# RWKV loop of a two-block model: rates, decays and products per chunk of 64 tokens instead of per block of 128

## The reference, cut to what matters

```python
def rwkv_prepare(rw, p):
    r, k, v, wl, al, gl = jnp.split(rw, RWKV_SPLITS, axis=-1)
    kk = heads(k * p['k_k'])                     # then normed per head
    w_lat = jnp.tanh(wl)
    for each direction:
        w = -jax.nn.softplus(-(w0 + w_lat @ w2)) - 0.5
        decay = jnp.exp(-jnp.exp(w))             # = exp(-exp(-0.5) * sigmoid(w0 + w_lat @ w2))
        a = jax.nn.sigmoid(a0 + al @ a2)
        k_dir = k * (1.0 + (a - 1.0) * p['k_a'])

def rwkv_scan(...):                              # for each direction
    def step(S, inp):
        sa = jnp.einsum('bhvk,bhk->bhv', S, kk_t)
        S = S * w_t - sa * (kk_t * a_t) + v_t * k_t
        return S, jnp.einsum('bhvk,bhk->bhv', S, r_t)
```

## Time and profile before

| | us |
|---|---|
| median of 3 runs (2999.21 to 3003.76) | 2999.66 |
| profiled execution | 3002.31 |
| its span | 3000.5 |
| TensorE busy in the span | 2717.9 (91%) |
| VectorE busy | 1418.4 (47%) |
| ScalarE busy | 516.1 (17%) |
| GpSimd busy | 162.8 (5%) |

### The profile page before, as it was taken

How to read it: one execution, slowest core, us unless ns; L and a number is a source line. 1 busy time by engine, 2 the same in 40 slices (tenths; PEclk the granted TensorE clock), 3 DMA queues, 4 the chain that set the end, 5 groups by cost and what they waited for, 6 DMA issues and landing times.

```text
span 3000.5 us, 46544 instructions
## 1 busy us (share of the span) xinstructions
PE 2717.9 (91%) x20206; PEld 1974.1 (66%) x20206; DVE 1418.4 (47%) x2486; ACT 516.1 (17%) x1033; POOL 162.8 (5%) x112
## 2 busy tenths in 40 slices
PE   7989999998999898999999988997778769999996
PEld 3643788886645445888884743546777733788885
DVE  3153655525004436555424365254444463877624
ACT  2121100001013322000001032013333211122100
POOL 0000000000000000000000000003333200000000
PEclk9979999999998989999999977997999979999998
DMA  5313222233120002232234101200000013222231
GB/s 189 97 36 98 71 85 85 67 100 100 57 84 1 1 30 83 93 96 84 58 99 128 42 15 56 56 1 2 4 4 4 4 57 98 71 85 84 67 91 53
DMA packets 219563, 190.34 MB, mean 63 GB/s; under 512 B 8667, under 2 KB 216956, under 8 KB 219360
## 3 DMA queue, kind: packets, MB, share of 16 engines
q1 hardware_dynamic: 219066, 187.27, 20.2%
q10 hardware_dynamic: 294, 0.09, 0.0%
HBM read 185.25 MB, written 2.10 MB: 62 GB/s over the span
## 4 chain that ended last, share of the span: by engine, by line
PE 81%; DVE 12%; issue 2%; ACT 2%; DVEq 0%; DMA 0%; POOLq 0%; POOL 0%; ACTq 0%; SPq 0%
PE psum L1138 26%; PE psum L335 18%; PE psum L1348 13%; PE psum L365 4%; PE psum L2041 4%; PE psum L2048 3%; PE psum L778 2%; PE psum L800 2%; DVE sbuf L277 1%; PE psum L786 1%; PE psum L776 1%; DVE sbuf L290 1%; PE psum L2118 1%; PE psum L1751 1%; DVE sbuf L2431 1%
## 5 line engine op out<-in xcount | busy, mean ns | idle before, releaser
L1138 PE MATMUL psum<-sbuf 128*128 128x256 f32 x3696 | 810.6, 383 | 9.9 <-DVE sbuf L1197 6.5
L1138 PEld LDWEIGHTS psum<-sbuf 128*128 128x128 f32 x3696 | 708.7, 192 | 110.8 <-DVE sbuf L1197 7.7
L335 PE MATMUL psum<-sbuf 128*128 128x512 f32 (+5 forms) x1424 | 542.4, 543 | 22.7 <-DVEq L434 22.5
L335 PEld LDWEIGHTS psum<-sbuf 128*128 128x128 f32 (+3 forms) x1424 | 264.5, 187 | 295.8 <-issue 257.1
L1348 PE MATMUL psum<-sbuf 128*128 128x256 f32 x1848 | 405.2, 382 | 12.4 <-DVE sbuf L1365 6.8
L1348 PEld LDWEIGHTS psum<-sbuf 128*128 128x128 f32 x1848 | 353.8, 192 | 63.5 <-DVE sbuf L1365 7.6
L1222 DVE TENSOR_TENSOR sbuf<-sbuf,psum 128x256 f32<-128x256 f32 x462 | 177.7, 415 | 205.7 <-PE psum L1138 204.5
L2048 PE MATMUL psum<-sbuf 64*64 64x64 f32 x4992 | 204.8, 232 | 32.6 <-issue 19.1
L2041 PE MATMUL psum<-sbuf 64*64 64x64 f32 (+1 forms) x4544 | 180.0, 233 | 50.3 <-DVE sbuf L2409 30.6
L2048 PEld LDWEIGHTS psum<-sbuf 64*64 64x64 f32 x4992 | 180.0, 143 | 44.2 <-issue 38.1
L2041 PEld LDWEIGHTS psum<-sbuf 64*64 64x64 f32 x4544 | 164.5, 141 | 57.1 <-DVE sbuf L2409 32.0
(11 more groups left out here) (232 smaller groups left out, 2516.7 us busy)
## 6 DMA issues: line engine op xcount, KB each, us to landing
sbuf<-in_w_mod_dram SPq DMA_DIRECT2D x24, 1024.0 KB, 5.2
sbuf<-in_w_ffn_gate_dram SPq DMA_DIRECT2D x22, 1024.0 KB, 5.5
sbuf<-in_w_ffn_up_dram SPq DMA_DIRECT2D x22, 1024.0 KB, 7.3
sbuf<-in_w_ffn_down_dram SPq DMA_DIRECT2D x32, 704.0 KB, 6.2
sbuf<-in_w_up_dram SPq DMA_DIRECT2D x22, 1024.0 KB, 5.4
sbuf<-in_w_out_dram SPq DMA_DIRECT2D x12, 1024.0 KB, 5.2
sbuf<-in_w_in_dram SPq DMA_DIRECT2D x12, 1024.0 KB, 5.3
sbuf<-in_w_down_dram SPq DMA_DIRECT2D x16, 704.0 KB, 6.3
```

What stands on the lines that cost most here:

```text
L335: mm = pe.matmul(bank, w[:, q, c0:c0 + m], rhs(k0 + q), start=start and q == 0, stop=stop and q == kc - 1)
L1138: mm = pe.matmul(bank, w[:, q, :], rhs[:, q, :], start=q == 0, stop=q == 3)
```

## The change

Preparation goes by chunk, both directions together, and three chunks ahead. Iterations n = -3, -2, -1 take the place of the separate prologue. In iteration n TensorE runs `latents(n + 3)` at the end of level 3 and `cums(n + 3)` at level 4, ScalarE `rate(n + 3)` and `exps(n + 3)` there, so every chunk has both. `latents` has two products of 512 columns, direction 0 into partitions 0 to 63 and direction 1 into 64 to 127 of bank 4, and eight of 64 columns. `cums` stays at four products of 256 columns, now for one chunk of both directions. `exps` has six exponentials of 256 elements in a main chunk instead of three of 512 for each block and direction. AR, B, K and GAM have buffers for four chunks. VectorE makes `products(n + 2)` as a generator and issues its instructions behind the updates of the levels: 5, 2, 1, 1, 1 of them. GpSimd's `kka` has two instructions of 256 elements and stands first in its iteration. `gram_l(g)` waits for the products of chunk g, made an iteration earlier. `kv`, `turn_v` wait for `exps` of chunk n + 2.

```diff
-        def latents(b, d):
-            tok = block_tokens(b, d)
-            pe.matmul(k.bank[4], WA[0:33, tok], W2A[0:33, d, :], start=True, stop=True)
-            for f in range(4):
-                mm = pe.matmul(k.bank[5][:, f * P:(f + 1) * P], W2A[64:97, d, f * P:(f + 1) * P], WA[64:97, tok],
-                               start=True, stop=True)
+        def latents(c):
+            if c >= 1:
+                wait("exps", c)
...
+            for d in range(2):
+                pe.matmul(k.bank[4][HEADS[d], :], WA[0:33, chunk_tokens(c, d)], W2A[0:33, d, :], start=True, stop=True)
+            for d in range(2):
+                for f in range(4):
+                    mm = pe.matmul(k.bank[5][:, column(4 * d + f)], W2A[64:97, d, f * P:(f + 1) * P], WA[64:97, chunk_tokens(c, d)],
+                                   start=True, stop=True)
             mm.then_inc(sems["latent_done"], 1)
...
         def gram_l(g):
-            wait("prods", prep(g // 2, 1))
+            wait("prods", g + 1)
...
-                if lv == 4:
-                    prepare(n, 1)
+                if lv == 4 and c < NCH:
+                    cums(c)
...
-                if lv == 3:
-                    if n == -1:
-                        wait("exps", 2)
-                    prepare(n, 0)
+                if lv == 3 and c < NCH:
+                    latents(c)
...
+        def exps(c):
+            wait("cums_done", c + 1)
+            cum = k.psum[:, 2048:3072].rearrange("p (f w d t) -> p f w d t", f=4, w=2, d=2)
+            for d in range(2):
+                incl, excl, tile = cum[:, :, 0, d], cum[:, :, 1, d], AR[c % 4][:, d]
+                act.activation(tile[:, :, 0, :], incl if d else excl, ACT.Exp, scale=-DECAY if d else DECAY)
+                act.activation(B[c % 4][:, d], excl if d else incl, ACT.Exp, scale=DECAY if d else -DECAY)
+                if main(c):
+                    act.activation(tile[:, :, 1, :], excl if d else incl, ACT.Exp, scale=-DECAY if d else DECAY)
+            act.activation(GAM[c % 4].unsqueeze(3), cum[:, :, 0, :, CH - 1:CH], ACT.Exp, scale=DECAY).then_inc(sems["exps"], 1)
...
+        def products(c):
+            Kf, Bf, rate, tile = K[c % 4], B[c % 4], RATE[c % 2], AR[c % 4]
+            flat4 = lambda ap: ap.rearrange("p d f t -> p (d f t)")
+            wait("exps", c + 1)
+            by_pair = lambda ap: ap.rearrange("p d f t -> p (d f) t")
+            dve.scalar_tensor_tensor(out=by_pair(Kf), in0=by_pair(rate), scalar=-1.0, in1=KA.unsqueeze(2).broadcast_to([P, 8, CH]),
+                                     op0=ALU.add, op1=ALU.mult).then_inc(sems["k_gain"], 1)
+            yield
+            for w, name in ((0, "KK"), (1, "R")):
+                for d in range(2) if w == 0 or main(c) else ():
+                    dve.tensor_tensor(tile[:, d, :, w, :], tile[:, d, :, w, :], src[name][:, :, chunk_tokens(c, d)], ALU.mult)
+                    yield
+            wait("k_gain", c + 1)
+            for d in range(2):
+                ins = dve.scalar_tensor_tensor(out=Kf[:, d], in0=Kf[:, d], scalar=1.0, in1=src["K"][:, :, chunk_tokens(c, d)],
+                                               op0=ALU.add, op1=ALU.mult)
+                if d == 0:
+                    yield
+            k.dve.link(ins)
+            yield
+            k.dve.link(dve.tensor_tensor(flat4(Kf), flat4(Kf), flat4(Bf), ALU.mult))
+            yield
+            wait("kka", c + 1)
+            dve.tensor_tensor(flat4(Bf), flat4(rate), flat4(Bf), ALU.mult).then_inc(sems["prods"], 1)
+            yield
...
                 if lv == 2 and 0 <= m < NCH - 1:
                     state(m)
-            if exps_in(n) is not None:
-                products(exps_in(n), 0)
+                for _ in range((5, 2, 1, 1, 1)[lv]):
+                    next(filler, None)
+            for _ in filler:
+                pass
```

## The result

The changed kernel takes 3008.52 us in the median (3003.02 to 3014.28, 10 runs), the kernel before 3000.64 (2997.03 to 3003.76, 10 runs): ratio 1.0026, 95% interval 1.0015 to 1.0036. It is slower; 2986 was predicted. The profiled execution after has a span of 3012.5 us, before 3000.5. It took 3014.28 us, the slowest of its ten and 5.8 us above the median, the one before 1.7 above, so about 4 of the 12.0 us are these two executions' own. The difference of 12.0 us lies in the prologue (+6.4) and the loop (+6.5), and the rest of the program is 0.9 us shorter.

The account below looks back on a forecast made before the run. TensorE was taken as the bound, stopped by VectorE's block of products. Terms -29.9 + 2 + 7.5 + 2 + 4.5 = -13.9 us took the median 2999.7 to 2986; own range 2979 to 2995 (chance 0.50), whole range 2972 to 3008.

Parts of the forecast that it names:

- Part 1: Loop, level-0 to level-1 and level-4 to level-0 updates: TensorE's stall behind VectorE's block of products goes, -29.9 us.
- Part 2: VectorE's products at their new places: level 0 costs +2 us (bounds 0 and +4), levels 1 to 3 cost 0.
- rival 1: Level 3, slower: B*rate is let in only after GpSimd's five loff instructions, +21 us, 3007; chance 0.18.
- rival 3: No change: K*B shows at level 2 (+5.6), the table switch at level 4 (+5), 2996.6 us; chance 0.15.
- Part 3: TensorE's latents and cums in the loop: 30.5 us before, 38.0 after, +7.5 (bounds -2.4 and +13.8).
- rival 2: TensorE's latents, faster: the two wide products share time, having different columns, 2974 us; chance 0.17.
- The upper bound: Case of Part 3: small latents follow behind the wide ones at 0.06 to 0.11 us each, +13.8 us.
- Part 4: ScalarE at level 4: exponentials come some 0.25 us late per main chunk, +2 us; the table load hides, 0.
- Part 5: Prologue, mostly at 1.2 GHz: latents and cums of its chunks cost more, +4.5 us (bounds +2 and +8).

Follow-up runs that it names:

- a_sched: Changed kernel with VectorE's products spread 5, 1, 1, 0, 2 over the levels instead of 5, 2, 1, 1, 1: 3004.66 us, ratio 1.0024 to the kernel before.
- a_quad: Changed kernel with each of its eight small latent products cut into two of 64 output channels: 2982.71 us, ratio 0.9950 to the kernel before.
- a_onetable: Changed kernel with the decays made by Sigmoid instead of Exp, no table switch in the loop (wrong numbers): 3011.16 us, ratio 1.0037 to the kernel before.
- a_lat_old: Changed kernel with old-shape latents per chunk, one 128-token product and four of 128 columns (direction 1 wrong): 2974.55 us, ratio 0.9917 to the kernel before.
- hybrid: Changed kernel with small latents as four products of 128 columns, one direction and two chunks at a time: 2993.07 us, ratio 0.9986 to the kernel before.

## Why the prediction was wrong, step by step

- **Part 1, the block goes (-29.9):** right. 29.1 us by the same four sums, no wait for the last product in the loop, the longest of the ten stretches U0 to U1 6.38 us.
- **Part 2, places on VectorE (+2):** wrong at level 1. "The second ends about when the next update is due: 0" holds only where TensorE is slow to bring that update. The half of K's product behind the eye takes up to 2.58 us, in chunks 0 and 1 (whose shorter list the prediction didn't count) B*rate 2.72, and in chunks 0 to 3 the update waits behind it: 11 us in U1 to U2. About 3 us come back in the next stretch, and in the medians of a_sched it can't be seen. Level 3 was right, and rival 1 is out: B*rate gets in between the five loffs of GpSimd and takes 1.38 or 1.39 us in all eight chunks where it stands there. VectorE, then GpSimd:

```profile
2266.33 1.38 DVE L2372 TENSOR_TENSOR sbuf<-sbuf 128x512 f32<-128x512 f32 x1
...
2265.90 6.61 POOL L2453 TENSOR_TENSOR sbuf<-sbuf 128x512 f32<-128x512 f32 x5 [9.11 <-DVE sbuf L2387]
```

  That rival 1's 3007 us lies near the measured 3008.5 is chance. At level 2 the sign of rival 3 is there: in six of eight chunks the evacuation starts within 0.1 us of K*B's end. What that cost can't be told from the rest.
- **Part 3, TensorE's preparation (+7.5):** this step failed, and it turned the sign. Taken were 2.3 us for a set of latents, wide ones in a row (they run side by side, as rival 2 had it) with the small ones beside them (they come behind, at 0.11 us a pass). The nine sets in the loop took 26.7 us, not 20.7. The upper bound, 9 x (3.0 + 1.92) = 44.3, had the latents right; what it left out is that the clock falls behind them, and that nine cums took 21.9 us, not 17.3. Together that is 48.6 us against the 30.5 taken for before, +18.1 for the +7.5 of the sum. U3 to U4 grew by 22.0 us; the rest would be TensorE's other products there at the lower clock. a_quad takes all of that away by the small products' width alone: 23 us by the ratios to the kernel before, and a kernel at 2982.7 us, near the forecast.
- **Part 4, ScalarE (+2):** not contradicted, a_onetable shows no gain from the switch, and elsewhere in the trace of before an instruction follows a table load at 0.01 us (899.96), so the 0.60 us was no time of the load. Rival 3's price for the switch is out.
- **Part 5, the prologue (+4.5):** +6.4 measured. Its own terms gave 1.4 + 3.8 = 5.2, of which 4.5 was taken without a reason; the rest is the same step as part 3, a set at 1.2 GHz being taken at 4.1 us and measured at 5.2 to 5.6 from the first start to the last end. With latents that overlap it is 35.18 us, 2.8 below the kernel before.
- **Sum.** With the latents side by side, rival 2 would have given 2974; a_quad is at 2982.7. In its profiled execution U1 to U2 is 10.2 us longer than before (73.26 for 63.06) and U2 to U3 4.2 shorter (60.2 for 64.4). That a_quad comes out near 2986 is in part luck, since it needs the wide products side by side, which the forecast had in a row.

What stays open: why the clock falls behind the sixteen small passes in six of nine chunks and not in the other three (in chunk 0 it was low shortly before the set as well, 0.58 over U2 to U3), and which part of the 33 us that a_lat_old gives is the clock's alone. By the estimate of 2 us a chunk it would be about 12 us, more than a third. Open is also what TensorE's stream takes back of a gain.

## What to carry to other kernels

When products are made smaller or moved, read from the trace which of them run beside each other, and ask whether the new shape keeps the weight widths of neighbours alike: equal widths overlapped, unequal ones queued, and 32 narrow passes were 1.8 us cheaper than 16 wide ones. A filler on VectorE that reads two operands from SBUF was free only where it started before GpSimd's next instruction (0.41 us, up to 2.58 behind it); the place is to be priced with GpSimd's whole duration. A stall that is taken away pays only as far as the engine that was stalled gets no dearer work in exchange, so the work moved has to be priced as closely as the stall.

## What the runs showed of the hardware that was not expected

- Passes with 33 rows and 128 columns of weights follow each other at 0.11 us, with 64 moving columns (after) as with 128 (hybrid).
- Transposes strung between products made a feature 0.44 us instead of 0.12, and the whole 81 to 90 us longer.
- TensorE's idle time called issue stands at fixed places of its stream, 256 instructions apart or a multiple of it, whatever the program does there: 38 to 55 us of a loop of 315 to 350. In the two runs with transposes, where TensorE itself is slower, it is 5 to 9 us of a loop of 423 to 427.
- GpSimd's five instructions in a row let one of VectorE's in between: 1.38 us instead of 0.69, in eight of eight chunks.
